# Routing and the first gather moved into the gate product, a gated embedding moved to GpSimd, and an expert pipeline rotated by three chunks

## The reference

```python
mix = concat([conv_out, attn_out]) @ w_out[i] + b_out[i]
h = layer_norm(DEEPNORM_ALPHA * h + mix, ln1_g[i], ln1_b[i])
if i % 2 == 0: f = swiglu(h, ffn_w1[j], ffn_w3[j], ffn_w2[j])
else:          f = moe_swiglu(h, w_router[j], moe_w1[j], moe_w3[j], moe_w2[j])
e = sigmoid(h @ ple_gate_w[i] + ple_gate_b[i]) * (p[i] @ ple_w[i])
h = layer_norm(DEEPNORM_ALPHA * h + f + e, ln2_g[i], ln2_b[i])
```

## Time and profile before

| | us |
|---|---|
| three runs | 2254.47, 2256.67 (median), 2260.68 |
| the profiled execution's own time | 2253.18 |
| its span | 2251.5 |
| PE busy | 2160.1 (96%) |
| DVE busy | 1548.4 (69%) |
| ACT busy | 1261.2 (56%) |
| POOL busy | 134.0 (6%) |

### The profile page before, as it was taken

The page is one execution under the profiler, slowest core; times in us unless marked ns, Lnnn a source line. Parts: engine busy times, 40 slices in busy tenths (PEclk is TensorE's granted clock), DMA queues, the critical chain, the costliest instruction groups (busy, mean ns, idle before and its releaser), DMA issues.

```text
span 2251.5 us, 30493 instructions
## 1 busy us (share of the span) xinstructions
PE 2160.1 (96%) x11395; PEld 1766.0 (78%) x11395; DVE 1548.4 (69%) x1337; ACT 1261.2 (56%) x1259; POOL 134.0 (6%) x145
## 2 busy tenths in 40 slices
PE   9999999998998999899799999999999999999987
PEld 8977797877866999775688787878787888878765
DVE  5756544556255554625488888888888888888897
ACT  6755443333243333333277767776777767776764
POOL 0022010000200000100000000000000000000240
PEclk9999999999999999999799999999999999999999
DMA  5522584123734555453299999999999999999984
GB/s 210 193 84 104 181 340 161 57 94 112 252 131 165 186 187 187 128 176 112 94 357 373 368 369 370 369 373 369 366 371 359 383 364 376 372 370 368 384 320 193
DMA packets 85452, 581.41 MB, mean 258 GB/s; under 512 B 9968, under 2 KB 9968, under 8 KB 19456
## 3 DMA queue, kind: packets, MB, share of 16 engines
q1 hardware_dynamic: 75728, 544.77, 64.6%
q0 software_dynamic: 9184, 34.54, 4.4%
q10 hardware_dynamic: 464, 1.02, 0.1%
HBM read 559.91 MB, written 15.73 MB: 256 GB/s over the span
## 4 chain that ended last, share of the span: by engine, by line
PE 86%; DVE 5%; DMA 2%; issue 2%; ACT 2%; POOL 1%; PEld 0%; ACTq 0%; POOLq 0%; DVEq 0%; SPq 0%; PEldq 0%
PE bank L562 76%; DVE wrest L2282 2%; DMA arena<-arena 2%; PE bank L1239 1%; ACT whi L1673 1%; POOL arena L480 1%; PE bank L763 1%; PE bank L895 1%; PE bank L790 1%; PE bank L1172 1%; PE bank L1039 1%; PE bank L893 0%; PE bank L1057 0%; PE bank L872 0%; PE bank L874 0%
## 5 line engine op out<-in xcount | busy, mean ns | idle before, releaser
L2282 DVE TENSOR_TENSOR wrest<-ring,whi 128x2048 fp32r<-128x2048 f32 x378 | 859.1, 2324 | 94.0 <-ACT whi L1673 93.9
L1673 ACT ACTIVATE whi<-ring 128x2048 fp32r<-128x2048 f32 x378 | 703.0, 1915 | 69.7 <-DMA ring<-in_w_moe 67.7
L562 PE MATMUL bank<-whi,xgT 128*128 128x512 f32 x1008 | 406.4, 403 | 14.9 <-DVE wrest L2282 14.9
L562 PE MATMUL bank<-wrest,xgT 128*128 128x512 f32 x1008 | 397.3, 394 | 0.0
L562 PE MATMUL bank<-whi,xgR 128*128 128x512 f32 x1008 | 394.4, 391 | 0.0
L562 PEld LDWEIGHTS bank<-whi,xgT 128*128 128x128 f32 x1008 | 190.1, 189 | 61.3 <-DVE wrest L2282 20.8
L562 PEld LDWEIGHTS bank<-whi,xgR 128*128 128x128 f32 x1008 | 190.1, 189 | 46.8
L562 PEld LDWEIGHTS bank<-wrest,xgT 128*128 128x128 f32 x1008 | 189.5, 188 | 39.0
L562 PE MATMUL bank<-whi,hidE 128*128 128x512 f32 x504 | 201.0, 399 | 7.3 <-DVE hidR L2287 5.5
L562 PE MATMUL bank<-wrest,hidE 128*128 128x512 f32 x504 | 198.0, 393 | 0.0
L562 PE MATMUL bank<-whi,hidR 128*128 128x512 f32 x504 | 196.7, 390 | 0.0
(11 more groups left out here) (418 smaller groups left out, 3750.9 us busy)
## 6 DMA issues: line engine op xcount, KB each, us to landing
ring<-in_w_moe SPq DMA_DIRECT2D x378, 1024.0 KB, 4.8
ring<-in_w_dense SPq DMA_DIRECT2D x135, 1024.0 KB, 4.9
row<-in_rows POOLq DMA_DIRECT2D x17, 512.0 KB, 7.8
xg_rows<-ncT POOLq DMA_DIRECT2D x12, 512.0 KB, 19.7
y_rows<-arena POOLq DMA_DIRECT2D x9, 512.0 KB, 7.0
arena<-xg_rows SPq DMA_DIRECT2D x9, 512.0 KB, 5.4
arena<-arena POOLq DMA_DIRECT2D x32, 142.0 KB, 7.4
arena<-in_tbias POOLq DMA_DIRECT2D x2, 1536.0 KB, 16.4
```

The lines of the kernel that those rows point to most:

```text
L562: ins = pe.matmul(out_, lhsT, rhs, start=start, stop=stop, **more)
L1673: S["w_hi"].on(a.activation(whi[:, n % HI_SLOTS, :], ring[:, c % RING, :], ACT.Copy))
L2282: S["w_lo"].on(v.tensor_tensor(wrest[:, s, :], ring[:, s, :], whi[:, n % HI_SLOTS, :].bitcast(F32), ALU.subtract))
```

## The change

1. Embedding. The gate product goes into banks 4 to 7. ACT first copies `p @ ple_w` out of these banks to SBUF (`ppx`). Bias (DVE) and sigmoid (ACT) go into `fe`; the product with `ppx` and the sum with alpha times h are six GpSimd operations (`embed`). PE no longer waits for `pg_in` and `ple_done` behind the gate product. In layer 1, bias and sigmoid come after the first three expert chunks.
2. Router. Logits are made transposed ahead of the gate product, in four groups of eight PSUM partitions, and turned back; ranks, and the gather of list 0, stand inside the gate product after its k steps 0, 2 and 4. DVE's rest of the last gate chunk is behind the choice of experts.
3. Expert chunks. ACT and DVE take chunks 0 to 2 of list 0 ahead of the loop, and in the loop n runs from 3 to 44, so the last three are the next list's; behind the last list three dummy chunks are loaded.
4. Between feed-forward and layer 1 ACT rounds the first chunk before it waits for `f_out`, PE does not wait for `f_added`, and some filler matmuls (`stay_awake`) are added there, at the start and before layer 0.

```diff
-START_FILL, POST_FILL, STACK_FILL, FF_FILL = 14, (6, 4), 3, (3, 3)
+START_FILL, POST_FILL, STACK_FILL, FF_FILL = (16, 3), (8, 6, 1), 3, (3, 4, 1)
+AHEAD = 3
...
+            for k in range(AHEAD):
+                sp.wait_ge(chunks_used.sem, n * E_CHUNKS + (N_DENSE - RING + k + 1))
...
+            def embed(i):
+                for j in range(2):
+                    wait(pool, "ple_act", 8 * i + 4 + 2 * j + 2)
+                    S["ple_done"].on(pool.tensor_tensor(fe[:, j, :], fe[:, j, :], ppx[:, j, :], ALU.mult))
...
+                    S["ple_done"].on(pool.tensor_scalar(ppx[:, j, :], h[:, j, :], ALPHA, None, ALU.mult))
...
+                    S["ple_done"].on(pool.tensor_tensor(fe[:, j, :], fe[:, j, :], ppx[:, j, :], ALU.add))
...
+            def route_logits():
+                for r in range(4):
+                    part = (hTh, hTr)[r % 2][:, :, :].bitcast(F32)
+                    for b in range(4):
+                        k = 4 * (r // 2) + b
+                        ins = pe.matmul(ps[0][32 * b:32 * b + 8, 0:SEQ], wrt[:, k, :], part[:, k, :],
...
+                        if i and k == 0:
+                            turn_logits()
+                        if i and k == 2:
+                            rank()
+                        if i and k == 4:
+                            gather_first()
...
-                wait(pe, "pg_in", 4 * (i + 1))
-                wait(pe, "ple_done", 4 * (i + 1))
...
-            wait(pe, "f_added", 4)
...
                         wait(pe, "m_ya", i + 1)
                         wait(pe, "m_yv", i + 1)
+                        wait(pe, "pg_in", 8)
...
-                else:
+                round_proj(i, 0)
+                if i:
                     wait(a, "f_out", FF_STEPS + 1)
...
-            round_gathered(0)
+            round_gathered(0, 2)
+            for n in range(AHEAD):
+                round_ahead(n)
+            gate_embedding(1)
             with a.Fori(0, n_iter) as i:
-                for n in range(E_CHUNKS):
+                for n in range(AHEAD, E_CHUNKS + AHEAD):
                     round_chunk(i, n)
-                    if n == 2:
+                    if n == 3:
                         copy_outputs(i)
...
+            for n in range(AHEAD):
+                rest_chunk(0, n)
...
+            bias_embedding(1)
...
             with v.Fori(0, n_iter) as i:
-                for n in range(E_CHUNKS):
+                for n in range(AHEAD, E_CHUNKS + AHEAD):
                     rest_chunk(i, n)
-                    if n == 1:
+                    if n == 3:
                         copy_outputs(i)
```

More of the change, by code:

```diff
@@ L688, in _ @@
             wait(pe, "small_split", 2)
+            wait(pe, "uT_lo", 1)
+            for _ in range(START_FILL[1]):
+                pe.matmul(ps[0][:, 0:L], ncT[:, 0:P], ncT[:, :], start=True, stop=True, skip_group_check=True)
             wait(pe, "uT_lo", KT)
@@ L1109, in layer @@
                 wait(pe, "hT_done", 4 * (2 * i + 2))
-                for m in range(GATE_CHUNKS):
+                if i:
+                    route_logits()
+                wait(pe, "ple_act", 8 * i + 4)
+                for m in range(GATE_CHUNKS - 1):
                     wait(pe, "w_lo", RESTS[i] + PROJ_CHUNKS + m + 1)
@@ L1131, in _ @@
                 if kind == "w2":
+                    if s == 0:
+                        wait(pe, "pg_in", 4)
                     if s == FF_STEPS - 1:
@@ L1632, in layer @@
                     round_dense(LAYER_FIRST[i] + GATE_AT + m, phi[m % 3], 3, LAYER_FIRST[i] + CONV_AT + 4)
+                for q in range(4):
+                    j, n = divmod(q, 2)
+                    wait(a, "pp_ps", 2 * i + j + 1)
+                    S["ple_act"].on(a.activation(ppx[:, j, n * 512:(n + 1) * 512], ps[4 + q][:, :], ACT.Copy))
                 copy_h(2 * i + 1)
@@ L2306, in add_last, with rest_gathered, rest_chunk, rest_hid @@
                 fin(v.tensor_tensor(f, f, ps[(0, 1, 4, 5)[2 * t + c]][:, :], ALU.add))
+            def rest_gathered(i, bank=6):
+                for b in range(2):
+                    x = slice(4 * b, 4 * b + 4)
+                    wait(v, "m_xga", 2 * i + b + 1)
+                    S["m_xgv"].on(v.tensor_tensor(xgR[:, x, :],
+                                                  ps[bank + b][:, :].rearrange("p (k n) -> p k n", k=4), xgT[:, x, :].bitcast(F32),
+                                                  ALU.subtract))
+            def rest_chunk(i, n):
+                wait(v, "w_hi", i * E_CHUNKS + (MOE_ROUNDED + n + 1))
+                s = (N_DENSE + n) % RING
+                S["w_lo"].on(v.tensor_tensor(wrest[:, s, :], ring[:, s, :], whi[:, n % HI_SLOTS, :].bitcast(F32),
+                                             ALU.subtract))
+            def rest_hid(i, j):
+                wait(v, "m_hT", i * E_STEPS + j + 1)
+                S["m_hr"].on(v.tensor_tensor(hidR[:, :, :], ps[4][:, :].rearrange("p (k n) -> p k n", k=4),
+                                             hidE[:, :, :].bitcast(F32), ALU.subtract))
             for j in range(2):
```

165 lines of the change are left out of this document (89 added, 76 removed).

## The result

The changed kernel takes 2301.02 us (median of 4 runs, 2299.24 to 2302.65), the kernel before 2258.68 us in the runs beside it: ratio 1.0186, 95% interval 1.016 to 1.0212, so it is slower. The forecast was 2289, with 2278 to 2298 as the likeliest case's own range and 2262 to 2302 as the range. The profiled execution has a span of 2301.0 us against 2251.5, which is 49.5 us more where 34.9 were forecast.

A forecast was written before the change was run, and what follows sets the result against it. PE, busy 96% of the span, was taken to bound the kernel. From 2253.2, gains of 38.5 and losses of 55.4 and 18 gave 2288.1, forecast as 2289 us; range 2262 to 2302, likeliest case 2278 to 2298.

The forecast's parts named there:

- List ends and clock: End of each list: PE waits for `hidR` behind three more rests, 55.4 us lost; 1.2 GHz behind nine waits, 18 more.
- Rival A: List ends: the clock holds through the repeated waits, 2270 us; chance 0.17.
- Rivals B and C: List ends: B, no wait, 2211 us, chance 0.09; C, DVE hides one or two of three rests, 2251, chance 0.07.
- The router: First gate matmul to list 0's first hidden transpose: gain 25.5 us, ends 20 and 33.
- Then it wants `m_yv`: List 0 before chunk 2: PE waits 5.2 us for the copy, behind bias, sigmoid and chunk 3's rest.
- Fillers and clock: Added filler matmuls in idle time: gain 0.5 us, between nothing and 2.5 us of clock.
- The feed-forward's own gain: Ahead of the feed-forward: PE's 5.08 us wait for bias and embedding goes; gain 6.5 us, ends 4 and 6.6.
- Feed-forward to layer 1: Between feed-forward and layer 1: DVE's first add and the normalization come earlier; gain 6 us, 4.1 at least, up to 7.0.
- GpSimd: `embed` at the router and feed-forward: six operations, 26 us, slow DVE's rests beside them to 4.28 us instead of 2.25.
- Rival D: GpSimd and the logits cost more, 10 us on top of the forecast, 2299 us; chance 0.10.

The follow-up runs named there:

- hid_first: The changed kernel with ACT's and DVE's work on the last hidden block and gathered tokens ahead of the next list's chunks 0 to 2: 2235.3 us.
- ahead_alone: The kernel before with only the expert loop turned (chunks 0 to 2 of list 0 ahead, three dummy chunks at the end): 2337.28 us, ratio 1.0343.
- list_fill: The changed kernel with seven filler products on PE behind the gathered transposes, ahead of the last hidden block's product: 2287.89 us, ratio 1.011.
- kept_early: The changed kernel with GpSimd's first signal `y_kept` given ahead of the second embedding and the scatters: 2285.21 us, ratio 1.0101.
- both: The changed kernel with the edits of hid_first and kept_early together: 2222.26 us, ratio 0.9829.
- copy_first: The changed kernel with the edits of hid_first and kept_early, and ACT's and DVE's copy of outputs ahead of chunk 3: 2214.75 us, ratio 0.9807.

## Why the prediction was right, and where its terms were off

| stretch | forecast | measured | worked out from |
|---|---|---|---|
| start to the last feed-forward product | -7.0 | -13.8 | 891.30 - 905.06 |
| from there to layer 1's first product | -6 | -7.5 | 12.30 - 19.85 |
| layer 1 up to the router | 0 | +0.7 | 139.99 - 139.32 |
| router to list 0's hidden transposes | -25.5 | -7.0 | 72.45 - 79.45 |
| from there to the end | +73.4 | +77.1 | 1184.96 - 1107.82 |
| sum | +34.9 | +49.5 | |

The forecast adds 0.9 us to the sum of 2288.1 for an execution that was 3.5 under the median; by its own reason 2291.6 would have stood there.

**List ends and clock: right.** Place, releaser and cause were as forecast, by three runs (hid_first, ahead_alone, list_fill). The wait was forecast at 7.2 us and is 6.95 in most lists; DVE's five rests end back to back there, so it was DVE's own work that counted, as said, with the DMA close behind (ACT's last rounding waited 0.53 us for it). The DMA did add to it in two lists of this execution, with waits of 8.81 and 9.11: there ACT waited 1.84 and 1.85 us for chunk 42 (1.23 in list 1), and DVE stood idle for 1.25 and 1.47 us before its rest. Why these chunks landed late is open; kept_early had waits of 6.95 to 7.31. A passage costs 7.7 us (129.6 - 121.9), with 8.1 forecast (6.6 - 0.5 + 2.0). Rival A fell: the clock did not hold. The Trainium skill's "TensorE: Matmul & The Clock Gate", section "HAM oscillation — how this bites in real kernels", says that a loop with such a wait in every pass starts every pass slow; the trace agrees, with 1.2 GHz around each of the nine waits, 0.51 in the window shown, and 1.00 in eight lists where fillers covered the wait. What it is worth was 2.0 us a list as far as PE's own products go, and 1.1 in the passage. Rivals B and C fell because DVE is at work without a pause up to `hidR` in most lists, with all three rests inside PE's wait.

**The router: the step that failed.** All that lies inside the gate product was right: from the first logit to the end of the gate product 29.05 us (1072.64 - 1043.59) where 28.5 were summed, no wait at ranks or gather. The loop's start cost nothing where I had 1.5. What failed is the sentence "Then it wants `m_yv`", and the list behind it: bias, sigmoid, chunk 3, copy. The copy has one more condition, `y_kept`, and it stood in the order of DVE that I had shown. I followed it on DVE and ACT but not to the engine that gives it. There the change had put six operations in front, 15.7 us, ahead of the scatters, which in the kernel before ran from 1118.04 on, ahead of the loop. With that condition met (kept_early) PE waited 5.28 us, and from the first logit to list 0's hidden transposes it took 54.0 us where 53.8 were forecast. Cost: 24.11 - 5.2 = 18.9 us, all of the miss of this stretch (-25.5 + 18.9 = -6.6, measured -7.0). That 5.28 meets 5.2 is in part luck: the rest of chunk 3 took 2.29 us and not the 4.28 that were priced, and it started 1.7 us later than summed, 1.28 of them a table load of ACT that the sum leaves out.

**Fillers and clock: mis-sized.** I gave them 0.5 us. About 5 are seen in the first 550 us (2.2 at the start, 2.6 ahead of layer 0). And layer 0's gate product, whose first 6 us ran at 1.2 GHz in the kernel before (first row), ran at full clock in the changed one (second row):

```profile
686.90:692.90 6.00, 5.99 (x14) 4.73 (x15) 0.00 (x0) 0.00 (x0) 0.00 (x0) 0.50 0.80 317
```

```profile
682.50:688.50 6.00, 5.92 (x26) 4.85 (x27) 0.02 (x1) 0.00 (x0) 0.00 (x0) 1.00 0.88 315
```

That is 12 products more in 6 us, 2.8 us. The feed-forward's own gain is then what was forecast: from layer 0's gate product to the last feed-forward product 9.4 us less (208.72 against 218.15), of them 6.6 where 6.5 were forecast. The 2.8 are not the fillers' doing, but chance as far as the profiles show: with the old fillers ahead_alone ran this stretch at 1.00, and with the new ones hid_first began it at 1.2 GHz:

```profile
684.35:690.35 6.00, 6.00 (x19) 4.80 (x20) 0.00 (x0) 0.00 (x0) 0.00 (x0) 0.72 0.87 311
```

I had looked for the slow clock only behind the waits that the change removes, not where it adds fillers.

**Feed-forward to layer 1: right, and a little over the upper end.** 7.5, with ends 4.1 to 7. The add came 2.2 us ahead of the last product, 2.4 were forecast.

**GpSimd: direction right, too dear.** The six operations took 20 us beside DVE's work, not 26, and 15.7 while DVE waited; rests beside them 3.35 to 3.7 us in the mean of two, not 4.28. The mean hides two kinds of rest. In the kernel both the one at 1088.79 took 2.48 us, and GpSimd's TENSOR_TENSOR, issued at 1089.08, ended 2.2 us behind it (1093.51); the next rest, issued at 1091.20, ended 2.2 us behind that (1095.66). So each waited for the whole of the other. A rest beside a TENSOR_SCALAR of GpSimd that was already running took its usual 2.29 us, as chunk 3's did in the changed kernel, kept_early, both and copy_first; a TENSOR_SCALAR issued during a rest waited like the others (4.69 us from 1093.60, against 2.77). Two of the six operations are of this kind, and the sum priced them like the four of list 8, which are all TENSOR_TENSOR. Rival D had looked for 10 us here. Its number, 2299, is the nearest to the measured time, but not its mechanism: slower rests cost nothing in the changed kernel, where PE was waiting anyway, and 3.9 us of waits once that wait was gone, and the logits took 1.85 us and not 5 more. What GpSimd did cost was the late signal. The Trainium skill's "SBUF — State Buffer", section "Who interferes with whom", has a DVE instruction with two SBUF inputs and a GpSimd instruction that reads SBUF block each other for whole instructions. The rows agree for GpSimd's TENSOR_TENSOR, to 0.1 us; by the 2.29 us of the rest of chunk 3 a TENSOR_SCALAR that was already running held no rest up.

So the number was inside the range by luck as well: misses of opposite sign met, 18.5 us too hopeful at the router and 3.7 behind it, 7.6 too cautious ahead of it, 14.6 in all (49.5 - 34.9), and of the 7.6 at least 2.8 are the clock of single executions. The direction was no luck: the list ends alone cost 77 us, twice the 38.5 of gains that were forecast.

## What to carry to other kernels

When work is taken round the end of a loop, place it behind whatever the current pass still waits for: the same three chunks cost 78 us in front of the last hidden block and about 7 behind it (0.6 a list and 2.6 at the end). When operations move to another engine, list every signal which that engine gives later in its program, and look up who waits for each; a signal that stood free can end up behind them. And before a copy that frees something is moved by two chunks, see what waits for it in each pass: one chunk earlier gave 1.17 us a list.

## What the runs showed of the hardware beyond what was expected

PE's idle time of 6.95 us in each list was enough for 1.2 GHz in each of them, though PE had been at work at full clock for over 100 us before. Five waits of 0.97 to 1.37 us within 22 us (list 0 of copy_first) left the granted clock at 1.00, as the window over them shows (below), while one of 1.91 us in list_fill was followed by 4 us at 1.2 GHz. Five more filler products ahead of layer 0, around idle times of 2 to 3 us, took away a stretch of 6 to 7 us at 1.2 GHz; five more at the start cut one of 10.2 us to 3.4 or to none. The clock also fell for 4 us or more where PE had no wait, at other places in each execution, and that makes most of the 10.6 us by which code that is alike differed ahead of the router. A rest of DVE and a TENSOR_TENSOR of GpSimd ran one after the other (2.48 us where the rest came first, 4.46 where it came second), while a rest beside a running TENSOR_SCALAR was not slowed (2.29). A list's passage repeated to 0.02 us where PE never waited long (hid_first, copy_first), and lay between 129.28 and 131.80 in the changed kernel.

```profile
1087.70:1109.10 21.40, 15.70 (x66) 11.35 (x64) 17.02 (x6) 16.17 (x13) 20.15 (x7) 1.00 0.75 267
```
